# Two attentions of a long kernel: transposes three tiles behind the scores, not two, and the value products later by one or two steps

## What is computed

```python
def mixer_a(h, hc, w_in, sinks, w_o, cos, sin, ctx_out):      # first attention: 16 heads in 4 groups, head size 64
    ...
    s_loc = jnp.where(valid, jnp.einsum('bqhgd,bkhd->bhgqk', qs, ks) * scale, NEG_INF)   # window of 128 keys
    s_ctx = jnp.einsum('bqhgd,bkhd->bhgqk', qs, kc) * scale
    p = jax.nn.softmax(jnp.concatenate([s_loc, s_ctx, sink], axis=-1), axis=-1)
    o = p_loc @ vs + p_ctx @ vc
    ...
    s = jnp.einsum('bqhgd,bkhd->bhgqk', qc, kc) * scale       # context queries read the context keys alone
    ...
    return (o * jax.nn.silu(g)) @ w_o, (oc * jax.nn.silu(gc)) @ w_o

def mixer_b(h, hc, w_in, q_norm_g, w_uq, kv_norm_g, w_ukv, w_o, cos, sin, ctx_out):
    ...                                                       # second attention: 16 heads, keys of 64 + 32 rotary
    s = (qn @ kn_all + qr @ kr_all) * scale                   # all 768 keys, 512 latent queries
    o = jax.nn.softmax(s, axis=-1) @ v_all
    return (o * jax.nn.silu(g)) @ w_o, ...
```

## Time and profile before

| | us |
|---|---|
| median of 3 runs | 2132.02 |
| lowest, highest | 2130.04, 2132.17 |
| profiled execution, its own time | 2129.73 |
| its span | 2127.9 |
| first attention, from its first scores to the output projection | 219.9 to 403.3 |
| second attention, the same | 577.4 to 789.7 |

### The profile page before, as it was taken

The page is one execution under the profiler, slowest core; times in us unless marked ns, Lnnn a source line. Parts: engine busy times, 40 slices in busy tenths (PEclk is TensorE's granted clock), DMA queues, the critical chain, the costliest instruction groups (busy, mean ns, idle before and its releaser), DMA issues.

```text
span 2127.9 us, 28226 instructions
## 1 busy us (share of the span) xinstructions
PE 2011.2 (95%) x10632; PEld 1569.2 (74%) x10632; DVE 997.5 (47%) x1770; ACT 878.3 (41%) x1664; POOL 698.5 (33%) x394
## 2 busy tenths in 40 slices
PE   5999999999999999999899999999998899999998
PEld 3888655688665567887677888887885477888886
DVE  3520778523366653378437435343116625525254
ACT  4322667424376654534453222225225643323233
POOL 1322122342100045331234444443442334444433
PEclk9999999999999999998899999999999999999999
DMA  8222333132100012230125333322331122333332
GB/s 297 60 66 63 100 100 109 51 104 65 40 1 1 1 30 88 71 90 31 42 82 156 127 99 94 104 90 73 106 107 51 44 78 80 109 98 93 99 92 84
DMA packets 209467, 174.36 MB, mean 82 GB/s; under 512 B 6080, under 2 KB 180775, under 8 KB 208183
## 3 DMA queue, kind: packets, MB, share of 16 engines
q1 hardware_dynamic: 206096, 163.86, 25.4%
q0 software_dynamic: 2192, 8.45, 1.2%
q10 hardware_dynamic: 1047, 0.26, 0.1%
HBM read 170.41 MB, written 7.38 MB: 84 GB/s over the span
## 4 chain that ended last, share of the span: by engine, by line
PE 80%; issue 7%; DVE 6%; ACT 4%; POOL 2%; SPq 1%; DMA 0%; POOLq 0%; DVEq 0%; ACTq 0%
PE ps L369 20%; PE ps L370 20%; PE ps L371 20%; PE ps L745 5%; PE ps L626 4%; PE ps L709 3%; POOL WL L1613 1%; PE ps L607 1%; DVE PT L727 1%; PE ps L690 1%; ACT PB L661 1%; SPq L1507 1%; PE ps L1129 1%; PE ps L1228 1%; DVE PB L649 1%
## 5 line engine op out<-in xcount | busy, mean ns | idle before, releaser
L1613 POOL TENSOR_TENSOR WL<-raww,WH 128x1024 fp32r<-128x1024 f32 (+1 forms) x247 | 583.0, 2365 | 909.6 <-ACT WH L321 832.7
L369 PE MATMUL ps<-HH,WH 128*128 128x512 f32 (+1 forms) x1368 | 522.4, 382 | 16.6 <-DVE HL L2580 7.8
L370 PE MATMUL ps<-HL,WH 128*128 128x512 f32 (+1 forms) x1368 | 518.6, 379 | 0.0
L371 PE MATMUL ps<-HH,WL 128*128 128x512 f32 (+1 forms) x1368 | 518.2, 379 | 0.0
L321 ACT ACTIVATE WH<-raww 128x1024 fp32r<-128x1024 f32 (+1 forms) x247 | 254.8, 1036 | 416.0 <-PE ps L371 411.3
L369 PEld LDWEIGHTS ps<-HH,WH 128*128 128x128 f32 x1368 | 259.4, 190 | 73.3 <-issue 17.5
L371 PEld LDWEIGHTS ps<-HH,WL 128*128 128x128 f32 x1368 | 259.0, 189 | 48.6
L370 PEld LDWEIGHTS ps<-HL,WH 128*128 128x128 f32 x1368 | 259.5, 190 | 46.6
L709 PE MATMUL ps<-ident,PB 128*128 128x128 f32 x952 | 157.7, 284 | 31.3 <-ACT PB L661 22.7
L709 PEld LDWEIGHTS ps<-ident,PB 128*128 128x128 f32 x952 | 109.4, 143 | 60.0 <-ACT PB L661 35.5
L661 ACT ACTIVATE PB<-PB,NB 128x512 f32<-128x512 f32 (+3 forms) x192 | 116.5, 607 | 73.1 <-DVE NB L649 70.2
(11 more groups left out here) (346 smaller groups left out, 3130.8 us busy)
## 6 DMA issues: line engine op xcount, KB each, us to landing
raww<-in_ffn_w_up SPq DMA_DIRECT2D x88, 512.0 KB, 3.8
raww<-in_ffn_w_down SPq DMA_DIRECT2D x40, 512.0 KB, 3.4
raww<-in_ada_w SPq DMA_DIRECT2D x32, 512.0 KB, 3.6
raww<-in_odd_w_in SPq DMA_DIRECT2D x24, 512.0 KB, 3.7
raww<-in_a_w_in SPq DMA_DIRECT2D x20, 512.0 KB, 3.8
raww<-in_even_w_in SPq DMA_DIRECT2D x17, 512.0 KB, 3.8
ADA<-in_ada_w SPq DMA_DIRECT2D x6, 1024.0 KB, 16.2
raww<-in_b_w_in SPq DMA_DIRECT2D x12, 512.0 KB, 3.9
```

What stands on the lines that cost most here:

```text
L369: nc.tensor.matmul(out, lh, rh, start=start and k == ks[0], stop=False)
L370: nc.tensor.matmul(out, lh, rl, start=False, stop=False)
L371: ins = nc.tensor.matmul(out, ll, rh, start=False, stop=stop and k == ks[-1])
L1613: nc.gpsimd.tensor_tensor(lo, raw_slot(k), hi.bitcast(F32), ALU.subtract).then_inc(*split_lo.mark(k))
```

## The change

Two numbers per attention become settings: `lag`, how many tiles the transposes come behind the scores, and `slots`, how many slots PB has. Their defaults are the old ones, 2 and 4. Both attentions get `lag` 3 and keep four slots, so PB is addressed as before (`prob` computes the same spans). All of a tile's later work follows: transposes and both copies come in step t + 3. The default `pv_plan` becomes (lag + 1, 4), so in the second attention the value products and `keep_o` come a step later, and so does the last pair of each. In the first attention the latent pairs get (5, 3) for (3, 4): they start two steps later in three pieces of two blocks, and `keep_o` comes one step later; the context pairs keep (5, 2). Reciprocals and spreads stay where they were. The third attention and the fourth keep the defaults.

```diff
@@ in build @@
-        PB = over("PB", 0, 4 * R)[:, :].rearrange("p (t n) -> p t n", n=R)
+        PBF = over("PB", 0, 4 * R)[:, :]
...
+        def prob(A, t):
+            w = 4 * R // A["slots"]
+            n = t % A["slots"]
+            return PBF[:, n * w:(n + 1) * w]
@@ att_max, att_exp @@
-            if t >= 4:
-                q, j = A["seq"][t - 4]
+            if t >= A["slots"]:
+                q, j = A["seq"][t - A["slots"]]
@@ att_pe, att_dve, att_act @@
-                q, j = att_at(A, t - 2)
+                q, j = att_at(A, t - A["lag"])
@@ finish_att @@
-            A.setdefault("pv_plan", lambda r: (3, 4))
+            A.setdefault("lag", 2)
+            A.setdefault("slots", 4)
+            A.setdefault("pv_plan", lambda r: (A["lag"] + 1, 4))
...
-                late, over_ = A["pv_plan"](r) if r + 1 < len(jobs) else (3, 1)
+                late, over_ = A["pv_plan"](r) if r + 1 < len(jobs) else (A["lag"] + 1, 1)
@@ ATT_A @@
-                                      "fill_pe": a_fill_pe, "fill_dve": a_fill_dve, "per": 4, "gate": a_gate,
+                                      "fill_pe": a_fill_pe, "fill_dve": a_fill_dve, "per": 4, "lag": 3, "gate": a_gate,
...
-                                      "pv_plan": lambda r: (3, 4) if r % 4 == 1 else (5, 2),
+                                      "pv_plan": lambda r: (5, 3) if r % 4 == 1 else (5, 2),
@@ ATT_B @@
-                            "score_wait": b_wait})
+                            "score_wait": b_wait, "lag": 3})
```

More of the change, by code:

```diff
@@ L641, in att_max @@
                 return
-            if t >= 4:
-                q, j = A["seq"][t - 4]
+            if t >= A["slots"]:
+                q, j = A["seq"][t - A["slots"]]
                 dve.wait_ge(*turned[A["name"], q, j, len(A["jobs"][q]["tiles"][j]["lots"]) - 1])
-            dst, src = PB[:, t % 4, 0:job["tiles"][i]["n"] * P], score_span(A, r, i)
+            dst, src = prob(A, t)[:, 0:job["tiles"][i]["n"] * P], score_span(A, r, i)
             if len(add.shape) == 3:
@@ L656, in att_exp @@
             fused = job["tiles"][i]["add"] is not None
-            if t >= 4 and not fused:
-                q, j = A["seq"][t - 4]
+            if t >= A["slots"] and not fused:
+                q, j = A["seq"][t - A["slots"]]
                 act.wait_ge(*turned[A["name"], q, j, len(A["jobs"][q]["tiles"][j]["lots"]) - 1])
-            dst = PB[:, t % 4, 0:job["tiles"][i]["n"] * P]
+            dst = prob(A, t)[:, 0:job["tiles"][i]["n"] * P]
             nc.scalar.activation(dst, dst if fused else score_span(A, r, i), ACT.Exp, bias=NB[:, r % 4, i:i + 1],
@@ L709, in att_turn @@
                     ins = nc.tensor.transpose(ps[:, b, q * P:(q + 1) * P],
-                                              PB[:, t % 4, (first + q) * P:(first + q + 1) * P], ident[:, :])
+                                              prob(A, t)[:, (first + q) * P:(first + q + 1) * P], ident[:, :])
                 ins.then_inc(*turned.mark(*key))
```

## The result

The changed kernel takes 2149.64 us (median of four runs, 2146.99 to 2154.25) against 2132.06 before: a ratio of 1.0086, 95% interval 1.0074 to 1.0098. It is slower by 17.6 us. Forecast were 2135.6, with a range from 2122 to 2143; the measured time lies above it.

A forecast was written before the change was run, and what follows sets the result against it. TensorE, busy 95% of the span, was taken as the bound, so only its waits count. First attention +3.0 and second +0.55 gave about +3.6 us on the median 2132.02: 2135.6 us, range 2122 to 2143.

The forecast's parts named there:

- steps 0 to 2: First attention: value products moved from steps 10 and 11 become unhidden, 2.35 us less 0.33 per period, +14.1 us in all.
- steps 3 to 7: First attention: TensorE's waits for VectorE's copies and before fillers go, -6.6 us; a new wait in step 4 costs +1.8.
- steps 8 to 11: First attention: without value products there, step 0 begins earlier, by 0 to 1.25 us per period, 5.9 us in sum.
- end, from step 8 of the last period: First attention: three value pieces without a wait replace four with one, but the projection waits for POOL's split; -0.4 us.
- Its rival: "The clock falls, 2155 us": emptied first-attention context steps drop TensorE to half clock, 7 x 2.7, about +19 us; chance 0.03.
- The new wait for bank 7: First attention, step 4: context value product waits for the later latent result, 0.45 us in four of seven periods, +1.8 us.
- The lock to VectorE's copy: First attention: step 11's transpose needs the bank read by VectorE's copy of step 10, limiting how early step 0 begins.
- the faster rival: 2123 us: context steps not locked to VectorE, moved products fill TensorE's idle time, waits saved in both attentions, -9; chance 0.31.
- slower, 2143: Rival: the locks cost as forecast in both attentions but most savings fail to come, about +11 us; chance 0.19.
- Second attention: Whole second attention: pair boundaries +0.7, start -0.3, end +0.15, together +0.55 us.
- The six boundaries between the pairs: Second attention: the `b_ql` wait goes, 1.1 us each, but a hidden value piece of 1.0 is exposed; together +0.7 us.
- the last boundary: Second attention, before the last pair: no keys to prepare and a spread that waits for nothing, so a full 1.0 us gain.

The follow-up runs named there:

- e5: Changed kernel plus 20 extra score products in steps 9 to 11 of each first-attention period; 2151.32 us, ratio 1.0096 to the kernel before, first attention 197.5 us.
- e1: First attention as in the changed kernel, second as in the kernel before; 2147.34 us, ratio 1.0075 to the kernel before, first attention 198.3 us.
- e13: Changed kernel plus 20 extra 128 by 128 transposes in steps 9 to 11 of each first-attention period; 2148.65 us, ratio 1.0082, first attention 196.8 us.
- e2: Second attention as in the changed kernel, first as in the kernel before; 2134.05 us, ratio 1.0007 to the kernel before, second attention 215.8 us.
- e17: Kernel before, with all value products of a second-attention pair in one piece (step 2 of 8); 2120.71 us, ratio 0.9937, second attention 201.1 us.
- e15: Kernel before, with second-attention value products in two pieces (steps 2 and 3 of 8); 2125.19 us, ratio 0.9971, second attention 205.0 us.
- e5b: Changed kernel plus 10 extra score products in steps 9 to 11 of each first-attention period; 2149.33 us, ratio 1.0092, first attention 196.0 us.

## Why the prediction was wrong

The forecast for the first attention was +3.0 us by steps; measured are +17.3. Summed over the periods, with e5 beside it, which had full clock but 160 products more:

| stretch | forecast | after | e5 |
|---|---|---|---|
| steps 0 to 2, seven times | +14.1 | +24.5 | +15.7 |
| steps 3 to 7, seven times | -4.8 | -2.5 | -2.5 |
| steps 8 to 11, with the start of the first period | -5.9 | -5.3 | -0.1 |
| end, from step 8 of the last period | -0.4 | +0.7 | +0.9 |
| sum | +3.0 | +17.3 | +14.0 |

**The clock: the step that failed.** The sum has no term for it: the forecast rests on full clock in both attentions. Its rival was there, priced at +19 us on top of the forecast, and given 3 in 100. Its mechanism came, with emptied context steps, half clock in and behind them, and value products of up to 1.7 times their length (3.29 us for 1.94). Its size was too high: steps 0 to 2 took 8.8 us more in after than in e5. Where the periods fell to half clock the difference is 7.0 us in four periods; the other 1.8 are small waits before the first piece (0.55 us in the second period), which comes earlier in after. The half clock adds some 0.4 before it, in the filler (1.08 us for 0.64). So the clock cost 7 to 9 us in this execution and some 2 less in e1: three falls at 2.0 to 2.1 us and one, at 261 us, at 0.8, not seven at 2.7. What was wrong was the chance. I set it low because every row of both attentions showed full clock. But those rows were of steps that had value products in them, and the very thing the change took away was this work. The third attention was the stretch shown that resembled the new state, and it was at half clock.

The prediction also cited the Trainium skill, page "TensorE: Matmul & The Clock Gate", section "Part 4: PE-mode transpose": transposes do not count as activity for the clock. It pointed to the right rival for a reason that the runs do not bear out: with 160 extra transposes, beside the products that stand there anyway, the first attention stood at 1.00 throughout (e13).

**Steps 0 to 2.** The price of the products out of hiding was 14.1 us and is 15.7 at full clock: right but for 1.6. A part of that is a slip: the two pieces of 1.0 and 1.45 us add up to 2.45, where the sum took 2.35, and seven times 0.10 are 0.7.

**Steps 3 to 7.** Forecast were savings of 6.6 against a new wait worth 1.8. The waits went as said, and its like, at 0.4 to 0.7 us in each of five periods; in the third and the sixth period these steps grew by 0.2 instead. The two waits before fillers (0.67 each) ended too, but they stood in step 2, under the value piece that is there now, and are counted in the row above. The new wait for bank 7 came in the four periods named, with 0.16 for 0.45 us. Together these steps gave 2.3 us less than the forecast.

**Steps 8 to 11.** Forecast -5.9, measured -5.3. The lock to VectorE's copy that I read off was right, and with it the answer to the faster rival: step 0 begins at most 1.3 us earlier behind step 8, 0.6 on average for the 0.85 forecast, and is in no period more than 2.0 earlier.

**The end** was to gain 0.4 and lost 0.7: the last latent product waited 0.53 for VectorE's copy, the next 0.43 for the scaled result, and the projection 0.68 for POOL's split.

Without the clock the first attention would have lost some 8 to 10 us, by these numbers. With the 3.5 us of the second that is 12 to 14 us, or 2144 to 2146: at or just past the end of the range. (Taken off the measured 2149.64 us, in which unchanged code came out shorter, it is 2141 to 2143.) So the clock is the largest miss and not the only one: of the 14.3 us by which the first attention missed its forecast, 5.6 stand in the four rows of the table at full clock (1.6, 2.3, 0.6 and 1.1), and the second attention missed by 3.0 more. The nearest rival is "slower, 2143", whose mechanism (the locks cost what they cost and the savings fall short) came as well. Its own terms, 10.0 us in the first attention and more than half of 7.0 in the second, make at least 13.5 us and not the 11 at which it was priced.

**Second attention.** Forecast +0.55, measured +3.5, the same in e2 at full clock. The start gave 0.5 (forecast 0.3). The six boundaries between the pairs cost 2.5 together for 0.7. The wait for `b_ql` went with 1.1 us each in its step, as said, and 0.2 in the next. But the products cost 1.4 a boundary for 1.0: steps 3 to 6 of the pairs grew by 0.85 + 2.04 - 0.64 - 0.86. The 1.0 was the hidden piece; 0.4 more came with the new neighbours of the pieces, and I can name no wait for it. The end cost 1.6 for 0.15. The order of time there, in after (it answers to the earlier trace rows):

```profile
802.35 1.27 POOL L1219 TENSOR_TENSOR b_ol<-ARENA,b_oh 128x512 fp32r<-128x512 f32 x1
...
802.59 1.31 DVE L686 COPY RB<-RCP 128x512 f32<-128x512 f32 x1
...
803.70 7.03 POOL L1620 TENSOR_TENSOR WL<-raww,WH 128x1024 fp32r<-128x1024 f32 x3
...
804.11 0.66 PE L695 MATMUL ps<-ident,RB 128*128 128x128 f32 x4 [0.39 <-ACT PT L734]
...
805.53 5.37 PE L750 MATMUL ps<-PT,ARENA 128*64 128x512 f32 x24 [0.76 <-ACT PT L734]
```

VectorE's copy starts ahead of POOL's splits and takes 1.31 us for 2.47; TensorE's last two waits end with ScalarE's tiles, so the copy held nothing up and the sum stands there. It still comes second, behind POOL's `b_ol`: that ends at 803.62, the copy 0.28 us later, and alone the same copy takes 0.43 (306.40 above). Before, it ended at 784.96, about 0.25 us behind the first of POOL's three splits, a third of 7.16 us from 782.32. The rule that the prediction took from the Trainium skill, page "SBUF — State Buffer", section "Who interferes with whom", by which the one that comes second waits the other's whole instruction out, agrees with both traces. The spread runs inside the wait, as forecast. The miss is in the last boundary, which was to gain 1.0 in full and lost 0.9 us; the tail behind it cost 0.6 more.

Of the signs set out ahead, the waits for ScalarE's tile (one of 0.5 us is left), the transposes of steps 10 and 11 behind VectorE, the wait of step 4 (0.16), `b_ql` from the third pair on and the spread that waits 1 us and more all came as written. None of them is a sign of the clock, and none was set for it.

## What to carry to other kernels

A step with idle time on the bounding engine is a place to hide work in, and it should be filled before any wait is removed elsewhere: here moving one hidden piece out of its place cost 1.4 us per pair and ate up the 1.3 us of wait that the move saved, while all the products in that place made the second attention 11.2 us shorter (e17: 2120.71 us, ratio 0.9924 to 0.9950, faster than both kernels).
When a change takes matrix products out of steps that also wait, price the clock by the stretches of the trace that look like the new state, not by the clock of the stretch as it is now. And look at the code behind the change too: a fall that is avoided at one place can come at another.
The same edit of a plan goes the other way in a stage with another bound: three and two pieces gained 4.5 and 7.3 us in the second attention and lost 5.1 and 13.9 in the first (clock falls included), so each stage wants its own run.

## What the hardware showed that I had not expected

TensorE's clock fell to 0.50 at 309.0 us of after, inside a wait of 1.99 us, and stayed there until about 315.8, though TensorE was busy without a break from 309.6 on.
160 extra matmuls or transposes, 17.6 us of TensorE by their slots of 0.11 us, made the first attention 3.3 and 4.0 us shorter than in after. The stage between the attentions, unchanged, grew by 2.0 us in both.
Cutting a run of value products into one more piece cost 0.34 to 0.37 us a pair (e15 against e17), with nothing to see of it in the waits.
A copy of VectorE that takes 0.43 us alone took 1.31 and 2.47 us beside POOL, and ended 0.3 us behind the POOL instruction that had started ahead of it.
What stays open: which of several gaps of the same length brings the clock down. After fell at four of seven, e5b at one. The whole times of one kernel spread by 1 to 10 us; the profiles of different kernels show half-clock stretches at different places of unchanged code, but that these make the spread is not shown.
